# A two-layer trunk with RWKV-7 time mixing: another order of work in the time mixing

## The reference

```python
def rwkv7_mixer(x, mu, w_rkv, w0, w1, w2, a0, a1, a2, g1, g2, k_k, k_a, r_k, ln_w, ln_b, w_out):
    xx = jnp.pad(x, ((0, 0), (1, 0), (0, 0)))[:, :-1] - x
    xrkv = x[None] + xx[None] * mu[:3, None, None, :]
    r, k, v = jnp.einsum('nbsd,nde->nbse', xrkv, w_rkv)
    xw, xa, xg = x + xx * mu[3], x + xx * mu[4], x + xx * mu[5]
    w_log = -softplus(-(w0 + tanh(xw @ w1) @ w2)) - 0.5
    decay = exp(-exp(w_log))
    a = sigmoid(a0 + (xa @ a1) @ a2)
    g = sigmoid(xg @ g1) @ g2
    kk = k * k_k, divided by its length in each head of 64
    k = k * (1 + (a - 1) * k_a)
    bh = kk * ah
    def step(state, inp):            # 256 steps, a 64x64 state in each of 16 heads
        sa = einsum('bhvk,bhk->bhv', state, -kk_t)
        state = state * w_t + sa * b_t + v_t * k_t
        return state, einsum('bhvk,bhk->bhv', state, r_t)
    yn = group norm of y over each head, times ln_w plus ln_b
    bonus = sum(rh * kh * r_k) * vh
    return ((yn + bonus) * g) @ w_out
```

## Time and profile before

| | us |
|---|---|
| median of 3 runs | 1398.32 |
| lowest, highest | 1397.29, 1409.79 |
| the profiled execution, its time | 1397.79 |
| its span, first to last instruction | 1396.0 |
| mean granted clock of TensorE, share of full | 0.888 |
| PE, DVE, ACT busy | 1235.0, 947.2, 551.0 |

### The profile page before, as it was taken

One profiled execution on the slowest core, in us unless ns is written; L12 is line 12 of the kernel. 1 busy time (PEld: TensorE's weight loads), 2 busy tenths in 40 slices (PEclk: granted clock), 3 DMA queues, 4 the chain that ended last, 5 costly groups with the idle time before them and its releaser, 6 DMA issues.

```text
span 1396.0 us, 20281 instructions
## 1 busy us (share of the span) xinstructions
PE 1235.0 (88%) x7950; PEld 981.2 (70%) x7950; DVE 947.2 (68%) x1291; ACT 551.0 (39%) x788; POOL 9.6 (1%) x27
## 2 busy tenths in 40 slices
PE   5799999973988899998999995958949998899998
PEld 2588887752547688886788884637828997688886
DVE  5888886886445888886888866856963246654443
ACT  2444444433342544446444444372312121443331
POOL 1000000000000000000000000000000000000000
PEclk9999999887559999999999997989965657999999
DMA  9788884850003888876688883304330120455550
GB/s 330 264 297 303 302 305 134 283 162 37 1 1 128 294 301 301 301 272 210 228 301 303 301 252 110 106 30 122 112 93 2 32 62 0 155 194 193 190 199 33
DMA packets 185852, 252.88 MB, mean 181 GB/s; under 512 B 30449, under 2 KB 121585, under 8 KB 185777
## 3 DMA queue, kind: packets, MB, share of 16 engines
q1 hardware_dynamic: 185778, 251.84, 53.7%
HBM read 249.71 MB, written 2.10 MB: 180 GB/s over the span
## 4 chain that ended last, share of the span: by engine, by line
PE 74%; DVE 14%; ACT 4%; issue 3%; DMA 3%; SPq 1%; POOL 0%; DVEq 0%; ACTq 0%; POOLq 0%
PE bank L696 19%; PE bank L698 19%; PE bank L697 19%; PE bank L1018 3%; DVE ada_acc L1693 2%; DVE gu_lo L1765 2%; PE bank L895 2%; PE bank L1130 1%; DMA front<-in_ada_w_dram 1%; PE bank L756 1%; PE bank L905 1%; PE bank L922 1%; DVE inv_tmp L2022 1%; DVE dn_lo L1775 1%; ACT gu_hi L1257 1%
## 5 line engine op out<-in xcount | busy, mean ns | idle before, releaser
L696 PE MATMUL bank<-gu_hi,xT_hi 128*128 128x512 f32 (+1 forms) x944 | 377.7, 400 | 35.3 <-DVE gu_lo L1765 9.1
L697 PE MATMUL bank<-gu_lo,xT_hi 128*128 128x512 f32 (+1 forms) x944 | 374.4, 397 | 0.0
L698 PE MATMUL bank<-gu_hi,xT_lo 128*128 128x512 f32 (+1 forms) x944 | 374.2, 396 | 0.0
L1765 DVE TENSOR_TENSOR gu_lo<-raw,gu_hi 128x2048 fp32r<-128x2048 f32 (+1 forms) x108 | 239.2, 2251 | 19.0 <-ACT gu_hi L1257 19.0
L696 PEld LDWEIGHTS bank<-gu_hi,xT_hi 128*128 128x128 f32 x944 | 182.7, 194 | 80.7 <-issue 18.9
L697 PEld LDWEIGHTS bank<-gu_lo,xT_hi 128*128 128x128 f32 x944 | 182.4, 193 | 39.4 <-issue 0.7
L698 PEld LDWEIGHTS bank<-gu_hi,xT_lo 128*128 128x128 f32 x944 | 182.4, 193 | 38.5
L1257 ACT CAST gu_hi<-raw 128x2048 fp32r<-128x2048 f32 (+1 forms) x108 | 199.9, 1881 | 17.4 <-DMA raw<-in_ffn_w_gu_dram 7.3
L1693 DVE SCALAR_TENSOR_TENSOR ada_acc<-ada_raw,cact,ada_acc 128x512 f32<-128x512 f32 x224 | 168.4, 752 | 11.8 <-DMA ada_raw<-in_ada_w_dram 0.7
L696 PE MATMUL bank<-dn_hi,hT_hi 128*128 128x512 f32 x320 | 136.4, 426 | 6.6 <-DVE dn_lo L1775 6.6
L1775 DVE TENSOR_TENSOR dn_lo<-raw,dn_hi 128x2048 fp32r<-128x2048 f32 x40 | 91.6, 2291 | 68.2 <-ACT dn_hi L1268 68.2
(11 more groups left out here) (281 smaller groups left out, 1321.9 us busy)
## 6 DMA issues: line engine op xcount, KB each, us to landing
raw<-in_ffn_w_gu_dram SPq DMA_DIRECT2D x176, 512.0 KB, 9.0
ada_raw<-in_ada_w_dram SPq DMA_DIRECT2D x128, 512.0 KB, 6.8
raw<-in_ffn_w_down_dram SPq DMA_DIRECT2D x40, 1024.0 KB, 5.0
raw<-in_rwkv_w_rkv_dram SPq DMA_DIRECT2D x24, 512.0 KB, 4.9
raw<-in_dsa_w_in_dram SPq DMA_DIRECT2D x16, 512.0 KB, 4.8
front<-in_ada_w_dram SPq DMA_DIRECT2D x8, 512.0 KB, 7.8
last_raw<-in_ffn_w_down_dram SPq DMA_DIRECT2D x4, 1024.0 KB, 6.1
raw<-in_dsa_w_out_dram SPq DMA_DIRECT2D x8, 512.0 KB, 5.5
```

What stands on the lines that cost most here:

```text
L696: nc.tensor.matmul(out_ap, sta_hi, mov_hi, start=start, stop=False, skip_group_check=True)
L697: nc.tensor.matmul(out_ap, sta_hi, mov_lo, start=False, stop=False, skip_group_check=True)
L698: return nc.tensor.matmul(out_ap, sta_lo, mov_hi, start=False, stop=stop, skip_group_check=True)
L1765: nc.vector.tensor_tensor(gu_lo[:, par, ks, 0:width], buf[:, i, 0:4 * width].rearrange("p (k c) -> p k c", k=4), gu_hi[:, par, ks, 0:width ...
```

## The change

Nothing is computed otherwise; instructions move, and some products are grouped in another way.

At the mixer's entry mix_w is made ahead of mix_k, with a semaphore step for each of its eight slices, so that `lora_in(0)` can follow slice by slice; `lora_out(0)` comes ahead of the first K projection, and `lora_out(1)` ahead of `project(K_BLOCK + 1, 0)`. On ACT the table for tanh is loaded first by an instruction without use, and both sets of sigmoids, then the exponentials, come ahead of the rounding of V's weights and the squares. On DVE the scan comes ahead of mix_g, mix_v and mix_r. PE, L941 to L979 before:

The products of 16 with `rp` (one chunk) are gone; those of 32 and 64 cover four chunks. On DVE `late_start`, `late_shift`, `late_gate`, `gate_scale` and one split stood ahead of the loop and now stand within chunks 0 to 3. The core of the diff:

```diff
-                for t, c in blocks:
-                    sp.dma_start(dram_block(0, t, c), sbuf_block(t, c)).then_inc(inv_saved, 16)
-                sp.wait_ge(inv_saved, 16 * len(blocks))
+                for c in range(4):
+                    sp.dma_start(dram_block(0, 0, c), sbuf_block(0, c)).then_inc(inv_saved, 16)
+                sp.wait_ge(inv_saved, 8 * 16)
...
-                    pe.wait_ge(mix_ready, i + 2)
                     for k in range(KD):
+                        if i == 0:
+                            pe.wait_ge(mix_ready, k + 1)
+                        elif k == 0:
+                            pe.wait_ge(mix_ready, KD + 2)
...
                 lora_in(0)
+                pe.wait_ge(lora2_in, 2 * 16)
+                pe.wait_ge(wa_hid_ready, 1)
+                lora_out(0)
                 project(K_BLOCK, 0, G)
                 lora_in(1)
                 project(K_BLOCK, 1, G)
-                pe.wait_ge(lora2_in, 2 * 16)
                 pe.wait_ge(wa_hid_ready, 2)
-                lora_out(0)
-                project(K_BLOCK + 1, 0, TB)
                 pe.wait_ge(wa_out, KD)
                 lora_out(1)
-                pe.wait_ge(mix_ready, 4)
+                project(K_BLOCK + 1, 0, TB)
+                pe.wait_ge(mix_ready, KD + 3)
...
+                ba(0)
                 pe.wait_ge(wa_hid_ready, 4)
                 project(V_BLOCK, 0, G)
-                ba(0)
                 pe.wait_ge(kd_ready, 1)
                 turn_k(1)
-                project(V_BLOCK, 1, G)
+                project(V_BLOCK, 1, G, range(0, 1))
                 ba(1)
+                project(V_BLOCK, 1, G, range(1, 2))
...
-                srcs = [negT, b_end, kdT]
+                srcs = [negT, kdT, b_end]
...
-                def wt(t, cc, into):
-
-                    rows = chunk_of(cc)
-                    for hh in range(RH):
-                        e, j = hh % 2, hh // 2
-                        mm = nc.tensor.matmul(into[half_of(e), j * CH:(j + 1) * CH], a_tok[rows, t, hs(hh)], inv[rows, t, hh, :],
-                                              start=True, stop=True, tile_position=(cc * CH, e * HD))
-                    mm.then_inc(wt_ready, 1)
+                def wt(t, into):
+
+                    for j in range(KD):
+                        for cc, dst in into:
+                            rows = chunk_of(cc)
+                            for e in range(2):
+                                hh = 2 * j + e
+                                mm = nc.tensor.matmul(dst[half_of(e), j * CH:(j + 1) * CH], a_tok[rows, t, hs(hh)],
+                                                      inv[rows, t, hh, :], start=True, stop=True,
+                                                      tile_position=(cc * CH, e * HD))
+                            if j == KD - 1:
+                                mm.then_inc(wt_ready, 1)
...
-                for cc, into in enumerate(bank[2:4] + TB):
-                    wt(0, cc, into)
+                wt(0, list(enumerate(bank[2:4] + TB)))
+                pe.wait_ge(wt_out, 4)
+                u0(1)
+                wt(1, [(0, bank[2]), (1, bank[3])])
...
-                    mm = outputs(t, 0, U, ys[t], [cc])
-                    if t == 1:
-                        mm = outputs(t, 1, v_tok, ys[t], [cc])
-                    if cc == 3:
-                        mm.then_inc(ys_ready, 1)
-                    if c == 0:
-                        pe.wait_ge(wt_out, 4)
-                        u0(1)
-                    if c < 4:
-                        pe.wait_ge(wt_out, 2 if c == 0 else c + 4)
-                        wt(1, c, bank[3])
+                    if c < 2:
+                        pe.wait_ge(wt_out, 6 + c)
+                        wt(1, [(2 + c, bank[3])])
+                    elif c == 2:
+                        pe.wait_ge(wt_out, 8)
+                        outputs(1, 1, v_tok, ys[1], range(0, 1), True)
+                    elif c == 3:
+                        outputs(1, 1, v_tok, ys[1], range(1, 2), True)
+                        outputs(0, 0, U, ys[0], range(0, 1))
+                    elif c == 4:
+                        outputs(0, 0, U, ys[0], range(1, 2)).then_inc(ys_ready, 1)
+                outputs(1, 0, U, ys[1]).then_inc(ys_ready, 1)
...
+                def save_inverse():
+
+                    act.wait_ge(ba_out, 4)
+                    for c in range(4):
+                        nc.scalar.dma_start(dram_block(0, 1, c), sbuf_block(1, c)).then_inc(inv_saved, 16)
+
+                def inverse_back():
+
+                    act.wait_ge(inv_stored, 16)
+                    for c in range(4):
+                        nc.scalar.dma_start(sbuf_block(1, c), dram_block(1, 1, c)).then_inc(inv_back[1], 16)
+
                 deviation(q, 1)
                 turned_tile(q, 1, plain=True)
                 act.wait_ge(g_ready[1], K_BLOCK)
+                nc.scalar.activation(stat[:, 9:10], stat[:, 8:9], ACT.Tanh)
                 round_half(K_BLOCK + 1, 0)
+                lora_hidden(0, hid_wa[0:WA, :], TB[0][0:WA, 0:SEQ], ACT.Tanh)
                 round_mix(MIX_K)
-                lora_hidden(0, hid_wa[0:WA, :], TB[0][0:WA, 0:SEQ], ACT.Tanh)
+                act.wait_ge(rwkv_in, 10 * 16)
+                lora_sigmoid(0, sigT)
                 round_half(K_BLOCK + 1, 1)
                 lora_hidden(1, hid_wa[P - WA:P, :], TB[1][P - WA:P, 0:SEQ], ACT.Copy)
-                act.wait_ge(rwkv_in, 10 * 16)
                 projected(K_BLOCK, G, lambda t: k_toks[0][:, t, :])
-                round_half(V_BLOCK, 0)
-                lora_sigmoid(0, sigT)
-                kk_squares(0)
+                lora_sigmoid(1, aT)
...
+                mix_in(3, mix_w, True)
                 mix_in(1, mix_k)
-                mix_in(3, mix_w)
                 rest_of_mix(MIX_K)
                 mix_in(4, mix_a)
                 rest_half(K_BLOCK + 1, 0)
-                mix_in(5, mix_g)
-                rest_half(K_BLOCK + 1, 1)
-                dve.wait_ge(lora_ready, 2)
-                mix_in(2, mix_v)
-                mix_in(0, mix_r)
-                rest_half(V_BLOCK, 0)
...
+                mix_in(5, mix_g)
+                rest_half(K_BLOCK + 1, 1)
+                dve.wait_ge(lora_ready, 2)
+                mix_in(2, mix_v)
                 dve.wait_ge(ln_in, 16)
                 kk_scaled(0)
+                mix_in(0, mix_r)
...
-                late_start()
-                late_shift()
-                late_gate()
-                gate_scale()
-                rest_of_block(RWKV_OUT0, 1, halves=range(1, 2))
...
-                    if c == 3:
+                    if c == 0:
+                        late_start()
+                    elif c == 1:
+                        late_shift()
+                    elif c == 2:
+                        late_gate()
+                    elif c == 3:
+                        gate_scale()
+                        rest_of_block(RWKV_OUT0, 1, halves=range(1, 2))
+                    elif c == 4:
...
```

129 lines of the change are left out of this document (68 added, 61 removed).

## The result

The changed kernel takes 1335.31 us in the median of four runs (1333.03 to 1338.01); the kernel before, with a fourth run added, 1403.62 in the median of its four (1397.29 to 1409.79). The ratio is 0.9505, with a 95% interval from 0.9461 to 0.9549: 5% faster. The profiled execution took 1335.42 us, with a span of 1333.7 and a mean granted clock of 0.911, against 1397.79, 1396.0 and 0.888 before. The forecast was 1339, range 1316 to 1356. Between the two medians the change is worth 68.3 us, where the forecast had 59: the time is 4 us off and the gain 9, since the forecast's base, 1398.3, lies 5 us under the median of the four.

What follows compares the result with a forecast made beforehand. PE was taken to bound the kernel, through idle holes and unexplained waits before the recurrence and too much work, mostly at 1.2 GHz, within it. -18.5 - 12.4 - 4.1 - 24 = -59.0 from 1397.8 gave 1339 us, range 1316 to 1356.

Steps and rivals of the forecast that it cites:

- Part 1: Entry to the end of the V projection: earlier mix_w and reordered queues give -18.5 us, bounds -12 and -21.
- Part 2: Inverse and pairs: the hole ahead of the pairs closes (-12.4 us) and unexplained waits in the pairs shrink (-4.1).
- The hole of 12.35 us: PE idle ahead of the pairs until DVE has scaled r; claimed to close whole, -12.4 us, bound -9.
- the 2.4 us that two queues were to save: Inverse's path to its load: eight DMA issues split over SP and ACT take half the time, 2.4 us less.
- I keep the other two and take -4.1: Pairs: of three unexplained waits (1.25, 1.90, 4.09 us) only the longest goes, -4.1, bounds 0 and -7.2.
- Part 3: Recurrence, 91.1 us before: regrouped read-out products, moved DVE work and interleaved wt give -24 us, bounds -17 and -43.
- 35.6 us of one-chunk products become three four-chunk ones at 3.6: Recurrence: one-chunk read-out products become three four-chunk ones, 10.8 us in all, -24.8 us.
- wt was priced at -1.5: Recurrence: wt(0), interleaving four row groups, goes from 5.86 us to 3.6 to 5.9, taken as -1.5.
- The recurrence warms up: Rival: the recurrence runs at a higher clock, -10 us more, or 1324 with ak's wait gone; chance 0.17.
- The entry pays half: Rival: DVE delivers mix_g and splits 5 to 7 us later, a projection waits, part 1 shrinks: 1352; chance 0.2.
- twenty-five: Slower rival: PE starved of instructions at 25 blocks of small records, 5.38 us each, 1461 us; chance 0.02.
- the prediction's own signs: Signs included pairs in 7 to 11 us, recurrence in 62 to 70; wrong if DVE ends waits inside the recurrence.

Runs made afterwards that it cites:

- gates-alone kernel: Kernel before with only the gate products ahead of the pairs, key transposes first and r scaled within the inverse: 1387.38 us, ratio 0.9884.
- the recurrence alone: Kernel before with only the new recurrence (four-chunk read-out products, interleaved wt, late_* in the loop): 1369.26 us, ratio 0.9750.
- one tile at a time: Changed kernel with read-out products issued one chunk after the other instead of four tiles in turn: 1369.75 us, ratio 0.9762 to the kernel before.

## Why the prediction came out right

**Part 1, -18.5 against -18.9: right.** The steps came where they were forecast: first product near 869 (869.59), transposes near 920 (921.31). sigT's sigmoid ended at 882.8 instead of near 881. PE was done with the second low-rank product at 880.4; it was ACT that ended this step. The first sixteen products took 6.62 us, not 5.7, so tanh came 1 us late, and behind it stood a rounding of mix_k (1.98), a table load (1.28) and the sigmoids (3.03). The three waits that it was to take away shrank to 3.69, 3.84 and nothing.

**Part 2, -16.5 against -12.8: the hole right, the rest wrong.** The hole of 12.35 us closed whole. The inverse started at 950.87, not near 947.6, and r was ready at 1004.5, not 998. The hole closed with 0.1 us left instead of 7. The inverse's start cost 3.3 us of it: the first store was issued 1.0 us later than forecast, and the 2.4 us that two queues were to save on the path did not come, since from the first store to the inverse's start it is 9.9 us as before. The 3.67 us that DVE waited for ACT's rounding cost the rest: that wait was not seen, though the diff moves the split one step ahead. The step that failed is "I keep the other two and take -4.1". It was right that the longest wait had to do with the loads that ran beside it: its instruction packet started 1.7 us after PE had stopped. But without them a wait stays there. The third wait shrank from 4.09 to 1.67 us and did not go, and the first was not kept but grew from 1.25 to 2.20: behind the gate products PE did some 140 products of the pairs in 1.5 us at full clock, where the 159 up to the first wait of before took 2.2 us at half clock, and stopped earlier against its packet. So the step gave -1.5 and not -4.1. The other miss is a cover that had no line in the sum: the gate products had kept PE at 2.4 GHz for the key updates behind them. Moved ahead, they left those updates at half clock and with two waits, +5.1 us, of which the bonus products (2.8) and gates (1.0) took 3.8 back. The gates-alone kernel shows the same 10.7 us for them, without the other edits.

The Trainium skill, Runtime: NRT & Kernel Launch, section Instruction fetch mechanics, has the refill of instructions, in blocks of 16 KiB or 256 instructions, hidden by the issue floor. The traces agree on the block (packets of 16 KB, 128 products with 128 weight loads from wait to wait) and not on the hiding: waits of 5.5 us stand in `ak` and 7.9 in pairs and key updates, in streams of the smallest products, and 1.1 where long products stand between. The prediction has the waits after 121, 100 and 99 recorded products; the trace has 159, 128 and 128. That the wait in `ak` would stay beside R's loads was right, 5.53 us.

**Part 3, -24 against -32.7: the mechanism right, the size off.** "35.6 us of one-chunk products become three four-chunk ones at 3.6" named the right term at too high a price: they took 7.1 us, since most ran at 2.4 GHz (1.09 to 1.42 us for 64 records). The removal is -28.5 instead of -24.8. wt was priced at -1.5 with a range up to its old time; it took 7.0 instead of 11.8, -4.8, and the chunk order alone explains wt(0), 2.05 against 5.86. The products with S and the update ran warmer, -6.0, which the forecast had at nothing and gave to the rival "The recurrence warms up". That rival was right in its mechanism: the clock was 0.75 over the stretch, 0.59 before. It is not the whole change that warms it; the recurrence alone does (0.71), and one tile at a time undoes it (0.52). Against these, waits grew from 4.9 to 10.6 us. They were priced at +1.6 in all. The largest, 3.03 us for ACT, was a chain that the prediction did not follow: the late split frees a buffer late, its load lands late, and ACT's rounding, which waits for it, stands ahead of the copy of U.

**The other rivals.** "The entry pays half" did not come: DVE was late nowhere for mix_g or a split that PE needed. Within the mixer PE ran short of instructions in seven places, with 13.8 us in all, where before it was 12.6 in four; not in twenty-five. Three of the prediction's own signs came out against it: the pairs took 12.1 us and not 7 to 11, the recurrence 58.4 and not 62 to 70, and DVE ended 5.4 of its 10.6 us of waits. The terms missed by -8.7 and +3.7, and what followed the mixer by 2: the time was 4 us off, its largest term 9. That the forecast came out so close is luck; that it named the three places and the mechanism of each is not.

## What to carry to other kernels

Small products on separate tiles of the array cost a fraction when they take turns, tile by tile, instead of finishing one tile first: loop over the tiles innermost, and wait to issue until several chunks are there. Before a long product is moved, look at what it covers: it can be what gives the fetch of PE's instructions its time, and what keeps the clock up for its neighbours. Mixed in between short ones it does both, and that was worth 10 us here. A wait that looks like a pure loss may cover other work; split it and see which wait is next. And a wait that no semaphore explains can be looked up among the DMA packets: if an instruction packet lands just ahead of its end, PE had run out of instructions.
